# The last attention rebuilt: compressed branch in four batches, wide units in fours, state-space input projected earlier

## The chip, the cores and the metric

The kernel runs on one core of a Trainium2 chip. The metric is the device time of the whole kernel in microseconds (us), from which the median of several runs is taken. Five engines work side by side: TensorE (PE in the profile; PEld are its weight loads), VectorE (DVE), ScalarE (ACT), GpSimd (POOL) and SyncE (SP); the last two only start transfers here. They are joined by semaphores: an instruction waits until a counter has reached a number, and adds to one when it ends. Each engine takes its instructions strictly in the order of the program.

## The reference, cut to what matters

Three layers work on 512 positions of width 1024. The first two (attention with a position bias, then spatial gating, each followed by a feed-forward block) are not touched. The third joins an attention of eight heads in two key groups with a state-space recurrence. Each head has three branches: compressed (31 pooled keys), selected and window. With 512 positions there are 8 blocks and 16 may be selected, and the window is 512 wide, so both wide branches come to ordinary causal attention over up to 512 keys.

```python
q, kcr, vcr, ksl, vsl, kwn, vwn, z_a, g_br, u, z_s = split(h @ w_in)
kc = rms_norm(compress(kcr)); vc = compress(vcr)              # 31 pooled keys
for each head, each query t:
    p0 = masked_softmax(q . kc * scale, cmp_end <= t)         # compressed
    p1 = masked_softmax(rope(q) . rope(k_slc) * scale, causal)
    p2 = masked_softmax(rope(q) . rope(k_win) * scale, causal)
    o = g0 * p0 @ vc + g1 * p1 @ v_slc + g2 * p2 @ v_win
attn = o * silu(z_a)
y = s5_mixer(u)                                               # state space
y = gelu(y); y = y * sigmoid(y @ glu_w + glu_b)
out = x + gate * (concat(attn, y * silu(z_s)) @ w_out)
```

## The kernel before, in words

All weights come as slabs of 128x2048 numbers, in a fixed list: SP loads them into two buffers `w_raw`, ACT rounds each to `w_hi`, DVE takes the rest as `w_lo`, and TensorE multiplies three times (hi.hi, lo.hi, hi.lo; the helper `three`, L449). A slab of a projection gives two tiles of 128x512, each by 24 matmuls. ACT and DVE prepare one slab ahead.

The third layer begins with the projections of q and of the keys and values, then the compressed keys: `blocks`, two pairs of slabs, a small network (`hdn`), `kc_full`, the normalized keys `kcT`. Between those stand the slabs of the two gates, z_a (tile `za`) and z_s (`zs`): four slabs, eight tiles. Then ACT takes the silu of both.

The attention is one loop of steps in each of three engines (`attention`), over `UNITS_H`: 96 units (head pair i, group g, block of 128 queries it, branch br), the branch innermost. Of every three units one is compressed (br 0, 32 keys) and two are wide (128 * (it + 1) keys). At step s TensorE does the scores of unit s into bank s % 3 (L620), the transposes of the weights of unit s - 3 (L630) and the product with the values of unit s - 4 (L641). DVE adds the mask and finds the maximum (L1474, into `h_s`), inverts the row sum (L1482), multiplies it with the gate (L1965, `wbr`) and adds the result into `h_o` (L1970, L1973). ACT copies the transposed weights of unit s - 3 (L1062) and takes the exponential of unit s (L1070).

Beside the loop stands the projection of the state-space input u: two slabs, four tiles, at steps 0, 22, 44 and 66 (`SIDE_H`, helper `side`), all through bank 7 (`ps[7]`), with twelve turns of u into the layout of the recurrence (`U_STEPS`, L853) through the same bank. Whoever uses bank 7 waits for `side_free`, which the reader of the use before it raises. POOL waits for the last of these uses, then loads the tables of the first block of the recurrence into the place of h (L429), and those of the second when the attention has ended (`ho_done`).

After the loop h_o is transposed (L608) and gated, then four blocks of the recurrence follow (L871 to L885), the gate matrix, and the output projection. The attention of the first layer uses the same helpers over 64 units (head, it), all of them wide, with side work at every fourth step up to step 28 and none after.

Of the kernel before, what the change touches and what calls it, by code (L numbers as in the profile page):

```python
# [40 lines left out]
S_HU = S_HCV + 4  # L41
S_HGLU = S_HU + 2
S_HOUT = S_HGLU + 1
N_SLABS = S_HOUT + 4
ADA_TILES = 48
# [27 lines left out]
def program(nc, I, out, tab_d, tz_d):  # L73
    ctx = ExitStack()
    with ctx:
# [91 lines left out]
        h_p = at("h_p", 48 * K, [P, 4, T])  # L167
        h_pt = at("h_pt", 56 * K, [P, 3, T])
        h_s = at("h_s", 62 * K, [P, 3, T])
# [12 lines left out]
        h_mask = at("h_mask", 88 * K, [P, T])  # L182
        placed[0] = 93 * K
# [3 lines left out]
        kcT = seq("kcT", [P, CMP_PAD])  # L187
        vc = seq("vc", [CMP_PAD, H_GROUPS, HD])
        wbr = seq("wbr", [P, 4])
# [7 lines left out]
        posT = seq("posT", [P, 2, 32])  # L197
        w2c = seq("w2c", [P, 2, 2, HD])
# [5 lines left out]
        glu_b = seq("glu_b", [P, 4])  # L204
        gT = seq("gT", [N_BR * H_HEADS, T])
        hT = seq("hT", [2 * CMP_PAD, 2, 256])
        assert placed[0] <= 109 * K, placed
# [39 lines left out]
        U = at("U", 68 * K, [NCH, GB, L * CH])  # L247
# [64 lines left out]
        UNITS_H = [(i, g, it, br) for i in range(4) for g in range(H_GROUPS) for it in range(TT) for br in range(N_BR)]  # L312
# [19 lines left out]
        SIDE_A, SIDE_H = Side([4 * u for u in range(2 * TT)], TT), Side([22 * u for u in range(4)], 2)  # L332
        U_STEPS = {start + d: (b, part) for b, start in enumerate(SIDE_H.starts) for part, d in enumerate((4, 8, 12))}
        U_USES = len(U_STEPS)


        @block.sync
        def _(sp):
# [12 lines left out]
            with sp.Fori(1, N_SLABS // 2) as i:  # L351
# [10 lines left out]
        def _(gp):  # L362
# [71 lines left out]
        def _(pe):  # L434
# [350 lines left out]
            for i in range(4):  # L785
                transposes([h_qr[:, t, i * P:(i + 1) * P] for t in range(TT)], "hx_full")
            pe.wait_ge(sem("hk_done"), 1)
            for i in range(2):
                transposes([h_kr[:, t, i * P:(i + 1) * P] for t in range(TT)], "hx_full")

# [19 lines left out]
            b = bank()  # L810
# [27 lines left out]
            def beside_h(s):  # L838
                side(SIDE_H, s, pair_h)
                if s not in U_STEPS:  # L840
                    return
# [1323 lines left out]
```

## Time and profile before

| what | value |
|---|---|
| runs | 2027.04, 2044.36, 2056.81 us (median 2044.36) |
| profiled execution, its own time | 2040.69 us |
| span in its trace | 2038.9 us |
| what lies around the span | 1.8 us |
| mean granted TensorE clock | 0.946 |
| PE busy | 95% of the span |
| last attention, first score to the transposes of its result | 1664.48 to 1893.15 us |

The span runs from the first to the last instruction. PE is called busy for nearly all of it, but a matmul at half clock counts as busy too, and takes about twice as long, so the granted clock has to be read beside the busy share.

### The profile page before, as it was taken

How to read it: one execution, taken by the hardware profiler on the slowest of the kernel's cores; microseconds unless marked ns; L12 is line 12 of the kernel's file. 1: busy time of each engine (PE TensorE's matmuls, PEld its weight loads, DVE VectorE, ACT ScalarE, POOL GpSimd, SP SyncE). 2: the span in 40 equal slices, each digit the busy share in tenths (PEclk: the TensorE clock that was granted, in tenths of full speed). 3: DMA queues.
4: the chain of work that ended last, by engine and by line, in shares of the span. 5: the costliest groups of instructions: out<-in, count | busy, mean ns of one | idle time of the engine just before them, and what ended most of it. 6: DMA issues, size and time to landing. Idle time of an engine off the chain costs nothing.

```text
span 2038.9 us, 25450 instructions
## 1 busy us (share of the span) xinstructions
PE 1928.8 (95%) x9553; PEld 1586.3 (78%) x9553; DVE 1185.2 (58%) x2640; ACT 683.9 (34%) x1170; POOL 102.3 (5%) x198
## 2 busy tenths in 40 slices
PE   3999999999999999989999999999999899999769
PEld 3887778888888887778888888888887776676667
DVE  5775564876476565564434587657757843354442
ACT  3323563523332342232323342233233243353121
POOL 0001110001000001100000000100110000000000
PEclk9999999999999999999999999999999995595779
DMA  8344321435333436622222333634532320001401
GB/s 332 125 145 155 101 97 63 143 111 183 126 135 106 165 145 225 218 93 91 82 96 83 109 127 132 221 110 142 176 114 96 110 104 1 21 1 65 176 39 62
DMA packets 44405, 246.05 MB, mean 121 GB/s; under 512 B 6080, under 2 KB 6304, under 8 KB 25728
## 3 DMA queue, kind: packets, MB, share of 16 engines
q1 hardware_dynamic: 23200, 153.26, 21.2%
q0 software_dynamic: 21088, 91.21, 13.4%
q8 instruction: 76, 1.25, 0.3%
q14 instruction: 41, 0.34, 0.0%
HBM read 229.23 MB, written 15.22 MB: 120 GB/s over the span
## 4 chain that ended last, share of the span: by engine, by line
PE 83%; DVE 10%; DMA 3%; ACT 2%; issue 2%; SPq 0%; DVEq 0%; ACTq 0%
PE ps L449 63%; PE ps L620 6%; PE ps L641 5%; PE ps L630 4%; DMA ada_raw<-in_ada 3%; DVE w_lo L1300 2%; PE ps L759 1%; DVE ada_raw L1328 1%; ACT w_hi L915 1%; DMA bv_g<-in_bv_g 1%; PE ps L871 1%; DVE pre L1421 1%; PE ps L883 1%; PE ps L706 1%; PE ps L884 0%
## 5 line engine op out<-in xcount | busy, mean ns | idle before, releaser
L1300 DVE TENSOR_TENSOR w_lo<-w_raw,w_hi 128x2048 fp32r<-128x2048 f32 x136 | 311.6, 2291 | 149.5 <-ACT w_hi L915 149.2
L915 ACT ACTIVATE w_hi<-w_raw 128x2048 fp32r<-128x2048 f32 x136 | 260.0, 1913 | 399.6 <-PE ps L449 376.9
L449 PE MATMUL ps<-h_hi,w_hi 128*128 128x512 f32 (+1 forms) x1008 | 380.7, 378 | 11.9 <-issue 4.8
L449 PE MATMUL ps<-h_lo,w_hi 128*128 128x512 f32 (+1 forms) x1008 | 376.0, 373 | 0.0
L449 PE MATMUL ps<-h_hi,w_lo 128*128 128x512 f32 (+1 forms) x1008 | 375.6, 373 | 0.0
L449 PEld LDWEIGHTS ps<-h_hi,w_hi 128*128 128x128 f32 x1008 | 193.0, 191 | 46.2 <-issue 6.4
L449 PEld LDWEIGHTS ps<-h_hi,w_lo 128*128 128x128 f32 x1008 | 192.6, 191 | 32.8
L449 PEld LDWEIGHTS ps<-h_lo,w_hi 128*128 128x128 f32 x1008 | 192.9, 191 | 31.5
L449 PE MATMUL ps<-hid_hi,w_hi 128*128 128x512 f32 (+1 forms) x576 | 211.3, 367 | 0.0
L449 PE MATMUL ps<-hid_lo,w_hi 128*128 128x512 f32 (+1 forms) x576 | 210.5, 366 | 0.0
L449 PE MATMUL ps<-hid_hi,w_lo 128*128 128x512 f32 (+1 forms) x576 | 210.5, 366 | 0.0
L449 PE MATMUL ps<-w_hi,h_hi 128*128 128x512 f32 (+1 forms) x480 | 184.7, 385 | 13.6 <-DVE w_lo L1300 7.0
L449 PE MATMUL ps<-w_lo,h_hi 128*128 128x512 f32 (+1 forms) x480 | 182.2, 380 | 0.0
L449 PE MATMUL ps<-w_hi,h_lo 128*128 128x512 f32 (+1 forms) x480 | 182.1, 379 | 0.0
L1328 DVE CUSTOM_DVE_ANT_0 ada_raw<-ada_raw,cond 128x1024 f32<-128x1024 f32 x108 | 131.1, 1221 | 70.7 <-DMA ada_raw<-in_ada 69.6
L449 PEld LDWEIGHTS ps<-hid_hi,w_hi 128*128 128x128 f32 x576 | 108.6, 189 | 17.7
L449 PEld LDWEIGHTS ps<-hid_lo,w_hi 128*128 128x128 f32 x576 | 108.6, 189 | 17.5
L449 PEld LDWEIGHTS ps<-hid_hi,w_lo 128*128 128x128 f32 x576 | 108.6, 189 | 17.4
L449 PEld LDWEIGHTS ps<-w_hi,h_hi 128*128 128x128 f32 x480 | 92.1, 192 | 32.5 <-issue 10.5
L449 PEld LDWEIGHTS ps<-w_hi,h_lo 128*128 128x128 f32 x480 | 91.9, 191 | 16.8
L449 PEld LDWEIGHTS ps<-w_lo,h_hi 128*128 128x128 f32 x480 | 92.0, 192 | 16.1
L1352 DVE SCALAR_TENSOR_TENSOR xT<-ps,mod,xT 128x512 f32<-128x512 f32 x64 | 47.6, 749 | 94.4 <-PE ps L449 94.1
(359 smaller groups left out, 2763.4 us busy)
## 6 DMA issues: line engine op xcount, KB each, us to landing
w_raw<-in_slabs SPq DMA_DIRECT2D x136, 1024.0 KB, 4.8
ada_raw<-in_ada POOLq DMA_DIRECT2D x108, 512.0 KB, 4.6
s_tables<-s_tab POOLq DMA_DIRECT2D x4, 2692.0 KB, 9.5
s_t<-s_tables POOLq DMA_DIRECT2D x4, 2692.0 KB, 9.5
ada_first<-in_ada SPq DMA_DIRECT2D x4, 1536.0 KB, 18.3
a_bias<-in_a_bias POOLq DMA_DIRECT2D x16, 256.0 KB, 3.0
xT<-in_xT SPq DMA_DIRECT2D x1, 2048.0 KB, 19.9
s_toeplitz<-KTp POOLq DMA_DIRECT2D x32, 64.0 KB, 3.5
```

Source lines behind the costliest of these rows:

```text
L449: last = mm(o, l, r, start=start and n == 0, stop=stop and n == 2)
L620: mm(ps[s % 3][:, 0:n], q, k, start=True, stop=True).then_inc(sem(pre + "s_full"), 1)
L630: last = nc.tensor.transpose(b[0:w, j:j + P], pt[:, u % 4, j:j + w], ident[:])
L641: last = mm(ps[5 + u % 2][:, 0:HD], pt[0:w, u % 3, j * P:(j + 1) * P], value(units[u], j), start=j == 0, stop=j == nb - 1)
L706: last = mm(norm_banks[t // 2][1][:, t % 2:t % 2 + 1], sq_x[:, k % 2, t * P:(t + 1) * P], ones[:, 0:1], start=k == 0 and t % 2 == 0, stop= ...
L759: last = mm(b[:, t * P:(t + 1) * P], b_v[:, t, gm * P:(gm + 1) * P], b_ws[:, gm // 3, :], start=True, stop=True)
L871: last = mm(b[:, g * NCH:(g + 1) * NCH], t["Gt"][:, g, q * P:(q + 1) * P], UT[:, blk * GB + g, :], start=True, stop=True)
L883: mm(o, UT[:, blk * GB + g, :], Tz[blk % 2][:, g, :], start=True, stop=False)
L915: A(w_hi[s][:], w_raw[:, s, :], ACT.Copy).then_inc(sem("hi_done"), 1)
L1300: tt(w_lo[s][:], w_raw[:, s, :], w_hi[s][:].bitcast(F32), ALU.subtract).then_inc(sem("lo_done"), 1)
L1328: V.tensor_tensor_reduce(out=w, in0=w, in1=cond[:, which, :], scale=1.0, scalar=0.0, op0=ALU.mult, op1=ALU.add, accum_out=mod_s[:, o:o + 1 ...
L1352: free(stt(xT[:, o, :], b[:], mod[:, g + o:g + o + 1], xT[:, o, :], ALU.mult, ALU.add))
```

## The change

It rebuilds the last attention and moves the slabs around it.

- The compressed branch leaves the units. `UNITS_H` becomes 64 wide units, four in a row with the same it (two branches, two groups). For each head pair i one batch (`compressed`) does the compressed branch for both groups and all 512 queries, in three parts at the steps of `CMP_STEPS`: scores against `kblk`, a matrix with the keys of the two groups in its two halves; two transposes; the product with `vblk`, the values laid out in blocks. All through bank 7. DVE does the softmax's sums for all eight query and group blocks at once, and adds the result to `h_o` at the steps of `CMP_ADD`.
- The scores of two units, the two groups, are issued together at every even step. DVE writes the masked scores into `h_p` itself, which has five places, so `h_s` is gone, and ACT's exponential works in place.
- The results of four units lie side by side in one bank. One reciprocal, one product with the gates (`h_w`), one multiplication and one addition serve all four.
- u is projected before the attention, where z_a and part of z_s were, and only three slabs stand there instead of four. The other half of z_a and all of z_s come beside the attention: three slabs, six tiles, at steps 1, 11, 22, 33, 44 and 55. SP's list `H_SLABS` gives the new order of loads.
- The silu of `za` is taken at step 13, that of `zs` after the attention. POOL's first load of tables waits for the last projection beside the loop (`H_READ`), its second for `h_added`.

```diff
-        UNITS_H = [(i, g, it, br) for i in range(4) for g in range(H_GROUPS) for it in range(TT) for br in range(N_BR)]
+        UNITS_H = [(i, it, br, g) for i in range(4) for it in range(TT) for br in (1, 2) for g in range(H_GROUPS)]
...
-        SIDE_A, SIDE_H = Side([4 * u for u in range(2 * TT)], TT), Side([22 * u for u in range(4)], 2)
-        U_STEPS = {start + d: (b, part) for b, start in enumerate(SIDE_H.starts) for part, d in enumerate((4, 8, 12))}
+        SIDE_A, SIDE_H = Side([4 * u for u in range(2 * TT)], TT), Side([1, 11, 22, 33, 44, 55], 2)
+        KCT_STEP = 4
+        U_STEPS = {step: (n // 3, n % 3) for n, step in enumerate((15, 16, 17, 19, 20, 21, 24, 25, 26, 28, 29, 30))}
+        CMP_STEPS = {step: (n // 3, n % 3) for n, step in enumerate((6, 9, 13, 23, 27, 31, 35, 38, 41, 46, 50, 57))}
+        CMP_ADD = {16 * i + 22: i for i in range(4)}
+        ZA_STEP = SIDE_H.starts[1] + 2
...
+            for n, slab in enumerate(H_SLABS):
+                sp.wait_ge(sem("lo_done"), S_HQ + n - 1)
+                sp.dma_start(w_raw[:, n % 2, :], I["slabs"][S_HQ + slab]).then_inc(sem(f"raw_in{n % 2}"), 16)
...
-                    gp.wait_ge(sem("side_free"), len(SIDE_A.starts) + len(SIDE_H.starts) + U_USES)
+                    gp.wait_ge(sem("side_free"), H_READ)
                 elif b == 1:
-                    gp.wait_ge(sem("ho_done"), NUH)
+                    gp.wait_ge(sem("h_added"), 4)
...
-            slab_t(H)
-            pe.wait_ge(sem("kcn_done"), 1)
-            transposes([kcn[:].rearrange("n g d -> n (g d)")], "kct_full")
-            pe.wait_ge(sem("acc_free"), c("bank"))
...
+            def compressed(i, part):
+
+                pe.wait_ge(sem("side_free"), base[0])
+                base[0] += 1
+                if part == 0:
+                    for it in range(TT):
+                        last = mm(ps[7][:, 64 * it:64 * it + 64], hq[:, i, it * P:(it + 1) * P], kblk[:], start=True, stop=True)
+                    last.then_inc(sem("c_full"), 1)
+                elif part == 1:
+                    pe.wait_ge(sem("c_exp"), i + 1)
+                    for h in range(2):
+                        last = nc.tensor.transpose(ps[7][:, h * P:(h + 1) * P], c_s[:, h * P:(h + 1) * P], ident[:])
+                    last.then_inc(sem("c_turned"), 1)
+                else:
+                    for h in range(2):
+                        last = mm(ps[7][:, 256 * h:256 * h + 256], c_pt[:, h, :], vblk[:], start=True, stop=True)
+                    last.then_inc(sem("c_out"), 1)
+
+            for s in range(NUH + 4):
+                if s < NUH and s % 2 == 0:
+                    i, it, br, _ = UNITS_H[s]
+                    n, ts = P * (it + 1), slice(it * P, (it + 1) * P)
+                    if s >= 2:
+                        pe.wait_ge(sem("hs_done"), s - 1)
+                    for g in range(H_GROUPS):
+                        r = slice(HD * g, HD * g + HD)
+                        last = mm(ps[(s + g) % 3][:, 0:n], hqr[r, i, ts], hk[r, br - 1, 0:n], start=True, stop=True)
+                    last.then_inc(sem("hs_full"), 1)
...
+                    for j in range(it + 1):
+                        last = mm(o, h_pt[:, u % 3, j * P:(j + 1) * P], hv[:, j, vc], start=j == 0, stop=j == it)
...
-            act.wait_ge(sem("z_copied"), 1)
-            A(za[:], za[:], ACT.Silu).then_inc(sem("z_done"), 1)
-            A(zs[:], zs[:], ACT.Silu).then_inc(sem("z_done"), 1)
...
+                if s == ZA_STEP:
+                    act.wait_ge(sem("side_free"), ZA_READ)
+                    A(za[:], za[:], ACT.Silu).then_inc(sem("za_done"), 1)
...
+            act.wait_ge(sem("side_free"), SIDE_ALL)
+            A(zs[:], zs[:], ACT.Silu).then_inc(sem("zs_done"), 1)
...
+                    step(tt(h_q4[:], ps[5 + q % 2][:, 0:256].rearrange("p (j d) -> p j d", d=HD),
+                            h_w[:, q % 2, :, :].rearrange("p b g -> p (b g)").unsqueeze(2).to_broadcast([P, 4, HD]), ALU.mult))
+                    tt(h_o[:, it, i * P:(i + 1) * P].rearrange("p (g d) -> p g d", d=HD), h_q4[:, 0:2, :], h_q4[:, 2:4, :], ALU.add)\
+                      .then_inc(sem("ho_done"), 1)
```

What the three engines then have in a row is shown at two places. The first is TensorE in the middle of the loop. Of before, the steps 8 to 10, where the units go from 384 to 512 keys (kcT and vc are compressed, hk and hv wide):

```order
L620 MATMUL ps<-hk,hqr 128x384
L630 MATMUL ps<-ident,h_p 128x128 x2
L641 MATMUL ps<-hv,h_pt 128x64 x2
L853 MATMUL ps<-ident,uT 64x128 x4
L620 MATMUL ps<-kcT,hq 128x32
L630 MATMUL ps<-ident,h_p 32x128
L641 MATMUL ps<-hv,h_pt 128x64 x2
L620 MATMUL ps<-hk,hqr 128x512
```

The same place of the changed kernel, steps 13 to 17 (vblk is the compressed batch, L852 are turns of u):

```order
L901 MATMUL ps<-hv,h_pt 128x64 x3
L871 MATMUL ps<-vblk,c_pt 128x256 x2
L882 MATMUL ps<-hk,hqr 128x512 x2
L891 MATMUL ps<-ident,h_p 128x128 x3
L901 MATMUL ps<-hv,h_pt 128x64 x3
L891 MATMUL ps<-ident,h_p 128x128 x4
L901 MATMUL ps<-hv,h_pt 128x64 x3
L852 MATMUL ps<-ident,uT 64x128 x4
L882 MATMUL ps<-hk,hqr 128x128 x2
L891 MATMUL ps<-ident,h_p 128x128 x4
L901 MATMUL ps<-hv,h_pt 128x64 x4
L852 MATMUL ps<-ident,uT 64x128 x4
```

The compressed units are gone from between the wide ones, two scores stand together, and turns of u stand at steps next to each other.

The second place is ACT at the beginning of the loop. Of before, from the root of the compressed keys' norm (kst) on:

```order
L1245 ACTIVATE kst<-kst,eps 32x2
L915 ACTIVATE w_hi_54<-w_raw 128x2048
L1249 ACT_TABLE_LOAD
L1249 ACTIVATE za<-za 128x2048
L1250 ACTIVATE zs<-zs 128x2048
L915 ACTIVATE w_hi<-w_raw 128x2048
L1070 ACT_TABLE_LOAD
L1070 ACTIVATE h_p,row_sum<-h_s,neg_max 128x32
```

Of the changed kernel, from the same instruction on, and further down around the silu of za:

```order
L1301 ACTIVATE kst<-kst,eps 32x2
L1333 ACT_TABLE_LOAD
L1333 ACTIVATE h_p,row_sum<-h_p,neg_max 128x128
L971 ACTIVATE w_hi_54<-w_raw 128x2048
...
L1320 ACT_TABLE_LOAD
L1320 ACTIVATE za<-za 128x2048
L1327 ACTIVATE h_pt<-ps 128x384
L1333 ACT_TABLE_LOAD
L1333 ACTIVATE h_p,row_sum<-h_p,neg_max 128x512
```

The two silus no longer stand ahead of the first exponential; one of them stands in the middle of the loop, with a table load on each side.

## Rows read from the trace of the kernel before

**Rows 1.** The page: engines' busy time, the granted clock in 40 slices, the chain.

```profile
PE 1928.8 (95%) x9553; PEld 1586.3 (78%) x9553; DVE 1185.2 (58%) x2640; ACT 683.9 (34%) x1170; POOL 102.3 (5%) x198
...
PEclk9999999999999999999999999999999995595779
...
PE 83%; DVE 10%; DMA 3%; ACT 2%; issue 2%; SPq 0%; DVEq 0%; ACTq 0%
```

**Rows 2.** Windows by stage: projections, last slab, last attention, rest (first row: columns).

```profile
core 0: us, PE busy (x) PEld busy (x) DVE busy (x) ACT busy (x) POOL busy (x), PEclk, DMA share, GB/s
...
1653.00:1664.50 11.50, 10.66 (x49) 8.47 (x47) 5.05 (x9) 3.60 (x4) 0.00 (x0) 1.00 0.26 93
1664.50:1893.15 228.65, 227.32 (x929) 157.72 (x929) 94.02 (x482) 98.45 (x309) 1.06 (x2) 0.68 0.07 24
1893.15:2038.90 145.75, 110.78 (x608) 97.83 (x608) 55.61 (x94) 24.83 (x30) 3.15 (x6) 0.84 0.25 97
```

**Rows 3.** Windows, same columns: the first attention, then where the clock fell or rose.

```profile
244.00:300.00 56.00, 56.00 (x325) 38.98 (x323) 37.65 (x154) 35.02 (x103) 7.46 (x14) 1.00 0.31 104
1672.00:1674.00 2.00, 1.49 (x6) 0.90 (x7) 1.39 (x11) 1.64 (x10) 0.00 (x0) 0.98 0.40 74
1674.00:1676.00 2.00, 2.00 (x7) 0.89 (x7) 0.28 (x1) 0.96 (x3) 0.00 (x0) 0.50 0.90 377
...
1724.00:1726.00 2.00, 2.00 (x8) 1.56 (x7) 0.00 (x0) 0.00 (x0) 0.00 (x0) 0.72 0.00 0
1738.00:1740.00 2.00, 2.00 (x10) 1.49 (x11) 1.64 (x10) 1.26 (x5) 0.00 (x0) 0.69 0.00 0
1778.00:1780.00 2.00, 2.00 (x6) 1.61 (x7) 1.97 (x3) 0.47 (x2) 0.00 (x0) 0.57 0.00 0
1840.00:1842.00 2.00, 2.00 (x14) 1.12 (x13) 0.98 (x7) 1.33 (x6) 0.22 (x1) 0.79 0.01 4
```

**Rows 4.** PE in order of time (start, us, instruction): first attention, one round of four.

```profile
252.96 0.49 PE L620 MATMUL ps<-a_kT,a_qT 64*128 64x128 f32 x2
...
259.60 0.48 PE L620 MATMUL ps<-a_kT,a_qT 64*128 64x128 f32 x2
```

**Rows 5.** PE in order of time, last attention: half clock, then full clock.

```profile
1693.61 0.63 PE L620 MATMUL ps<-kcT,hq 64*128 64x32 f32 x2
...
1715.41 0.63 PE L620 MATMUL ps<-kcT,hq 64*128 64x32 f32 x2
...
1789.43 0.40 PE L620 MATMUL ps<-kcT,hq 64*128 64x32 f32 x2
...
1790.50 0.60 PE L853 MATMUL ps<-ident,uT 128*64 128x128 f32 x4
1791.03 0.49 PE L620 MATMUL ps<-hk,hqr 64*128 64x128 f32 x2
...
1802.94 0.36 PE L620 MATMUL ps<-kcT,hq 64*128 64x32 f32 x2
```

**Rows 6.** PE in order of time: start of the attention, side work begun at half clock.

```profile
1652.30 0.50 PE L449 MATMUL ps<-h_hi,w_hi 128*128 128x512 f32 x1
...
1664.48 0.40 PE L620 MATMUL ps<-kcT,hq 64*128 64x32 f32 x2 [0.84 <-DVE kcT L1952]
1664.82 0.50 PE L449 MATMUL ps<-h_hi,w_hi 128*128 128x512 f32 x1
...
1670.48 0.71 PE L620 MATMUL ps<-hk,hqr 64*128 64x128 f32 x4
...
1720.50 0.80 PE L449 MATMUL ps<-h_hi,w_hi 128*128 128x512 f32 x1
...
1728.29 1.12 PE L620 MATMUL ps<-hk,hqr 64*128 64x512 f32 x2
```

**Rows 7.** ACT in order of time: start of the attention, side copy, after the attention.

```profile
1664.29 1.92 ACT L1249 ACTIVATE za<-za 128x2048 f32<-128x2048 f32 x1 [7.35 <-DVEq L1950]
...
1669.82 1.28 ACT L1070 ACT_TABLE_LOAD   x1
...
1728.40 0.60 ACT L1038 ACTIVATE uT<-ps 128x512 f32<-128x512 f32 x1 [7.22 <-PE ps L449]
...
1910.31 0.59 ACT L1262 ACTIVATE y_nat<-ps 64x512 f32<-64x512 f32 x1 [9.66 <-PE ps L885]
```

**Rows 8.** POOL in order of time: the loads of the first two tables.

```profile
1841.78 0.54 POOL L429 DMA_DIRECT2D s_t<-s_tables  x1 [336.59 <-ACT UT L1046]
...
1893.39 0.53 POOL L429 DMA_DIRECT2D s_t<-s_tables  x1 [50.54 <-DVE h_o L1973]
```

**Rows 9.** Groups of PE's instructions, 244 to 300 us: the scores (busy us, mean ns).

```profile
L620 PE MATMUL ps<-a_kT,a_qT 64*128 64x512 f32 (+3 forms) x66 | 26.8, 486 | 0.0
```

More of the change, by code:

```diff
@@ L789, in _ @@
                 transposes([h_kr[:, t, i * P:(i + 1) * P] for t in range(TT)], "hx_full")
+            for i in range(4):
+                transposes([h_qr[:, t, i * P:(i + 1) * P] for t in range(TT)], "hx_full")
             for kind in range(2):
@@ L809, in _ @@
             pe.wait_ge(sem("hdn_done"), 2)
-            b = bank()
+            pe.wait_ge(sem("acc_free"), c("bank"))
+            wait(pe, "side_free", base[0])
+            base[0] += 1
             for kind in range(2):
@@ L836, in pair_h, with turn_u @@
                 return ps[7][:], (w_hi[sl][:, cols], w_lo[sl][:, cols]), (h_hi[:, k, :], h_lo[:, k, :]), False
[L838 to L841, printed above, removed]
-                b, part = U_STEPS[s]
+            def turn_u(b, part):
                 pe.wait_ge(sem("side_free"), base[0])
@@ new lines, in _ @@
+            for s in range(NUH + 4):
[8 more added lines that the diff above has]
+                    last.then_inc(sem("hs_full"), 1)
+                u = s - 3
+                if 0 <= u < NUH:
+                    n = P * (UNITS_H[u][1] + 1)
+                    pe.wait_ge(sem("hp_ready"), u + 1)
+                    if u >= 2:
+                        pe.wait_ge(sem("hpt_ready"), u - 1)
+                    for j in range(0, n, P):
+                        last = nc.tensor.transpose(ps[3 + u % 2][:, j:j + P], h_p[:, u % 5, j:j + P], ident[:])
+                    last.then_inc(sem("ht_full"), 1)
+                u = s - 4
+                if 0 <= u < NUH:
+                    i, it, br, g = UNITS_H[u]
+                    pe.wait_ge(sem("hpt_ready"), u + 1)
+                    if u % 4 == 0 and u >= 8:
+                        pe.wait_ge(sem("ho_done"), u // 4 - 1)
+                    o, vc = ps[5 + u // 4 % 2][:, (u % 4) * HD:(u % 4 + 1) * HD], slice((br - 1) * P + g * HD, (br - 1) * P + (g + 1) * HD)
+                    for j in range(it + 1):
+                        last = mm(o, h_pt[:, u % 3, j * P:(j + 1) * P], hv[:, j, vc], start=j == 0, stop=j == it)
+                    last.then_inc(sem("ho_full"), 1)
+                side(SIDE_H, s, pair_h)
+                if s == KCT_STEP:
+                    pe.wait_ge(sem("kcn_done"), 1)
+                    pe.wait_ge(sem("side_free"), base[0])
+                    base[0] += 1
+                    nc.tensor.transpose(ps[7][:, 0:CMP_PAD], kcn[:].rearrange("n g d -> n (g d)"), ident[0:CMP_PAD, 0:CMP_PAD])\
+                      .then_inc(sem("kct_full"), 1)
+                if s in U_STEPS:
+                    turn_u(*U_STEPS[s])
+                if s in CMP_STEPS:
+                    compressed(*CMP_STEPS[s])
@@ L1976, in _ @@
-            attention(UNITS_H, lambda u: CMP_PAD if u[3] == 0 else P * (u[2] + 1), mask_h, combine_h, "h", SIDE_H)
-            c.add("slab", 2)
-            c.add("full", 2)
-            dve.wait_ge(sem("z_done"), 2)
-            dve.wait_ge(sem("ho_done"), NUH)
+            kc = ps[7][0:CMP_PAD, :].rearrange("n (k g d) -> n k g d", k=4, d=HD)
+            step(cp(kcn[:], kc[:, 0, :, :]), *[cp(vblk[CMP_PAD * r:CMP_PAD * (r + 1), r, :], kc[:, 1, r % 2, :]) for r in range(4)])
+            V.engine_nop().then_inc(sem("side_free"), 1)
@@ L1981, in _ @@
+            c.add("slab", 3)
+            c.add("full", 3)
+            dve.wait_ge(sem("za_done"), 1)
             for i in range(5):
```

199 lines of the change are left out of this document (131 added, 68 removed).

## Prediction

> **What bounds the kernel now.** I read the page first [rows 1]: PE is busy for 95% of the span and makes up 83% of the chain that ended last, so the time is set by what PE is given and how fast it runs it. The slices of the granted clock are nines except for a run near the end, 5595779. The windows by stage [rows 2] say what that run is: the last attention, 228.65 us, in which PE is busy for 227.32 us at a mean granted clock of 0.68. DVE (94.02) and ACT (98.45) are far from being the bound there. With two levels, 1.00 and 0.50, a mean of 0.68 means that 64% of the stage ran at half clock. So there are two ways to make this stage shorter: less work for PE, or the same work at full clock. The change touches both. The slab ahead of the loop, 11.50 us at 1.00, belongs to the place as well. The rest, 145.75 us, does not change.
>
> Then I looked at where the clock moves [rows 3]. It fell at about 1674, after a start with waits on PE (0.84 us in front of the first score [rows 6]); it rose near 1725, some 4.5 us into the side work that began at 1720.50; it fell again near 1739, some 10 us after that work; it rose near 1780, again during side work, and fell once more in the window at 1840. Between the side works nothing raised it. But the first attention, 56 us of which are in [rows 3], has no side work there and is made of wide units alone, and it holds 1.00. So in the last attention it is not the lack of side work by itself that costs the clock; the narrow compressed units, a third of its units, are the plain difference.
>
> **PE's work after, at full clock.** Wide units: one round of four of the first attention (128, 256, 384, 512 keys) takes 259.60 - 252.96 = 6.64 us [rows 4]. The changed loop has 64 wide units with the same mix, 16 rounds: 106.2 us. As a check on before: nine units took 1802.94 - 1789.43 = 13.51 us at full clock with three turns of u, and 21.80 at half clock with one [rows 5]. A turn is 1791.03 - 1790.50 = 0.53; without turns that is 11.9 against some 20.8 (one turn of 0.95 taken off), a factor of 1.76, by which I price half clock below. Side work: 1670.48 - 1664.82 = 5.66 us at full clock, 7.79 when begun at half [rows 6]; six of them are 34.0 us. Two are new inside the loop, and the slab of 11.50 us ahead of it is what they replace, so this is a move and no saving. Turns: 12 x 0.53 = 6.4 us, as before. Compressed batches: no row shows one. It is four scores, two transposes and two products. From below, each costs no more than one 32-key score (0.36 [rows 5]): 8 x 0.36 = 2.9 us; from above, the two products, of 256 columns each, cost twice that: 3.6. I take 3.0, since scores and transposes are as short as in that row and the products stream only a little longer; 12 us for four, 11.6 to 14.4 for the range. They replace 32 compressed units, whose scores alone cost more than 32 x 0.36 = 11.5. kcT: 0.3. The sum is 106.2 + 34.0 + 6.4 + 12.0 + 0.3 = 158.9 us.
>
> **Waits.** The first score starts when the slab ahead of it is gone. Before, that slab ran from 1652.30, and kcT with its wait came behind it, to 1664.48 [rows 6]. After, the network's product goes to bank 7 and waits for the copy of the last slab's tile, below 1 us, so I start the loop at 1653.2. The start: before, ACT spent 1.92 us on the silu of za at 1664.29, as much on zs, and 1.28 on a table load at 1669.82 [rows 7], all ahead of the first exponential. Now the two silus are gone from there, and what stays is mask, table load, exponential, copy: I put 3 us on PE for this. The silu of za at step 13 costs ACT 1.28 + 1.92 + 1.28 = 4.5 us, with copies and exponentials queued behind it. The exponentials run three steps ahead of the transposes, and three steps of 384 to 512 keys are over 5 us, so I cost it at nothing, 2 us if that cover is short. The silu of zs falls into ACT's idle 9.66 us before 1910.31 [rows 7]: nothing. POOL's first load of tables moves from 1841.78 to behind the side work of step 55; 12 steps follow, over 20 us, and its wait in POOL's queue has nothing behind it but the second load, which is issued at the end as before, at 1893.39 [rows 8]. Nothing. SP's new order of slabs keeps two buffers and the same spacing of one slab per 22 steps. Nothing.
>
> Bank 7 is now used by turns, batches, kcT and side work, 31 times against 16. Each user waits for the reader of the one before. The reader of a side use before was ACT, 0.60 us at 1728.40 [rows 7]; turns of u stand at neighbouring steps, so one read has a step to be done in, and a step is 6.64 / 4 = 1.7 us. Bounds: 0 and 0.6 us for each of the 31, or 0 to 19; I take 4, since most have a step or more between them. At the end the last four results need two DVE operations and the addition of the compressed part before h_o can be turned: 1.5 us. Waits: 3 + 4 + 1.5 = 8.5, range 3 to 25.
>
> **The clock.** With 159 us of work and 1.00 throughout, the stage would be 167.4 us. The first attention says that wide units hold the clock [rows 3]; side work now comes every 11 steps, some 18 us, and before it raised the clock each time. But the start has waits again, and before, the clock fell there. And three places (steps 16 to 21 and their like) put scores of 128 keys, turns and batches close together. I take two stretches at half clock, each until the next side work, about 10 us of full-clock work: 10 x 0.76 = 7.6 us, and 7.79 - 5.66 = 2.1 for the side work begun at half, 9.7 each, 20 in all. The stage is then 187 us at a mean clock of about 0.88.
>
> **Sum.** Loop from 1653.2 to 1653.2 + 187.4 = 1840.6, against 1893.15: 52.5 us less. The profiled execution took 2040.69, so 1988. The median of the runs shown is 2044.36, 0.2% above it, which is below what a measurement tells apart; 2% here is 41 us.
>
> **A rule on the scores.** No row shows the scores of the two groups next to each other, each on one half of the array's rows. The scores take 26.8 of 56 us in the first attention [rows 9], so 3.2 us of a round and 51 in all; two at once throughout would save 25 us, none nothing. Every score is two instructions (x2 in [rows 4]), in order, so only the second of one and the first of the next can meet: a quarter, 13 us. In my sum they are in series, since the trace shows no other case. The Trainium skill, TensorEngine Tiling (Array Packing), section Key Properties, says that different tiles can execute weight loads and matmuls in parallel; by that rule the sum would be some 1975, and nothing in this case's trace bears on it yet. It is the third rival.
>
> **Rivals.**
> - The clock holds throughout. For it: the first attention [rows 3]. Against: its banks and queues were not shared with turns and batches. 20 us less: 1968. Chance 0.17.
> - Half clock as often as before, 64% of the stage. For it: the clock stayed down for 50 and 40 us between rises [rows 3], the start still waits. At 1.76 the 167.4 us of work and waits become 167.4 / (1 - 0.64 x 0.432) = 231, the end 1884: 2032, no change that can be told. Chance 0.15.
> - The scores overlap: 13 us less than the forecast, 1975, and with a clock that holds 1955. Chance 0.17.
> - Slower: bank 7 becomes the chain. Its 31 uses each cost a full round trip, TensorE to the reader and back, behind exponentials in ACT's queue or in DVE's; at 2.5 us each that is 78 us, PE idles, and the clock stays down: 231 + 78 - 4 = 305, less 240 from 1653.2 to 1893.15, gives 65 more, 2106. From about 1.7 us for each use, with the clock down, it is slower by over 2%. Against: the one read shown took 0.60 us [rows 7] and a step is longer. Chance 0.05.
> - The forecast, one to three stretches at half clock, 1978 to 2003: chance 0.46.
>
> **How the numbers follow.** Faster by over 2% (below 2003) are the forecast, the first and the third rival, less the upper edge of the forecast's bounds (waits to 25 us, batches at 14.4): 0.74. Within 2% are the second rival and that edge: 0.21. Slower: 0.05. The range holds all but the slow rival, most of the second, and the overlap with a held clock: 1960 to 2024.
>
> **What the trace after would show.** The first score near 1653; the transposes of h_o near 1841; a stage of 187 us at a clock near 0.88, low at the start and in one place further on; rounds of four at 6.6 us where the clock is full; no wait of PE for ACT at step 13 or for POOL's tables; waits for bank 7 below 0.6 us each; the rest at 146 us. Two scores of different groups that begin within less than their length would show the overlap. I am wrong if the clock stays at 0.50 between side works although the narrow units are gone, or if PE shows waits of over a microsecond for bank 7.

## The result and the profile after

The changed kernel takes 1942.38 us (median of four runs, 1941.69 to 1943.64) against 2042.61: a ratio of 0.956, 95% interval 0.951 to 0.961. It is faster, as forecast, but by about 99 us between the two profiled executions (2040.69 and 1941.69) where 52.5 were forecast, and the time lies below the range, 1960 to 2024.

The page after, in the parts that answer to [rows 1]:

```profile
PE 1823.2 (94%) x9449; PEld 1525.6 (79%) x9449; DVE 1154.1 (59%) x2392; ACT 669.9 (35%) x1086; POOL 101.9 (5%) x198
...
PEclk9999999999999999999999999999999999999789
...
PE 80%; DVE 11%; DMA 4%; ACT 2%; issue 2%; SPq 0%; DVEq 0%; ACTq 0%
```

PE is as busy as before by its share (94%), and the bound as before. But the slices of the clock that read 5595 in [rows 1] are nines now. The windows by stage after, with the columns of [rows 2]: up to the first score, the last attention up to the transposes of its result, the rest.

```profile
1560.00:1656.49 96.49, 88.40 (x462) 71.69 (x461) 72.88 (x95) 25.52 (x22) 0.00 (x0) 0.98 0.31 113
1656.49:1795.53 139.04, 129.92 (x875) 101.83 (x873) 68.03 (x243) 85.11 (x226) 1.06 (x2) 1.00 0.13 47
1795.53:1939.90 144.37, 109.85 (x608) 97.42 (x608) 55.53 (x94) 27.86 (x32) 3.14 (x6) 0.85 0.26 98
```

The stage takes 139.04 us at 1.00, where 187.4 at about 0.88 were forecast. The rest is 144.37 us against 145.75 [rows 2]. So the whole surprise lies in this one stage. PE in order of time shows half of it (start, duration, instruction; x4 are the two scores of a pair, two instructions each):

```profile
1743.43 0.92 PE L882 MATMUL ps<-hk,hqr 64*128 64x384 f32 x4
1744.28 0.44 PE L891 MATMUL ps<-ident,h_p 128*128 128x128 f32 x2
...
1749.05 1.13 PE L882 MATMUL ps<-hk,hqr 64*128 64x512 f32 x4
1750.11 0.55 PE L891 MATMUL ps<-ident,h_p 128*128 128x128 f32 x3
```

Start to start, two scores of 512 keys take 1750.11 - 1749.05 = 1.06 us and two of 384 keys 0.85. In the kernel before, one score of 512 keys at full clock took 1788.33 - 1787.28 = 1.05 us:

```profile
1787.28 1.12 PE L620 MATMUL ps<-hk,hqr 64*128 64x512 f32 x2
1788.33 0.55 PE L630 MATMUL ps<-ident,h_p 128*128 128x128 f32 x3
```

Two scores now cost what one did.

PE's idle time in the stage is 139.04 - 129.92 = 9.1 us, where I had put 8.5 of waits. The rows with the longest waits (the bracket: idle before, and who ended it):

```profile
1657.95 0.47 PE L465 MATMUL ps<-h_hi,w_hi 128*128 128x512 f32 x1 [0.97 <-DVEq L2027]
1664.95 0.70 PE L882 MATMUL ps<-hk,hqr 64*128 64x256 f32 x4 [0.64 <-DVE neg_max L2039]
1686.28 0.88 PE L901 MATMUL ps<-hv,h_pt 128*128 128x64 f32 x6 [0.85 <-ACT h_pt L1327]
1688.78 0.88 PE L901 MATMUL ps<-hv,h_pt 128*128 128x64 f32 x6 [1.18 <-ACT h_pt L1327]
1702.70 0.47 PE L465 MATMUL ps<-h_hi,w_hi 128*128 128x512 f32 x1 [1.40 <-ACT UT L1102]
1795.53 2.82 PE L624 MATMUL ps<-ident,h_o 128*128 128x128 f32 x16 [1.64 <-DVE h_o L2101]
```

And what ACT does ahead of the two waits near 1687: the silu of za between two table loads.

```profile
1681.43 0.49 ACT L1327 ACTIVATE h_pt<-ps 128x384 f32<-128x384 f32 x1 [0.94 <-PE ps L891]
...
1682.64 1.28 ACT L1320 ACT_TABLE_LOAD   x1
1683.94 1.91 ACT L1320 ACTIVATE za<-za 128x2048 f32<-128x2048 f32 x1
1685.76 0.47 ACT L1327 ACTIVATE h_pt<-ps 128x384 f32<-128x384 f32 x1
1686.24 1.28 ACT L1333 ACT_TABLE_LOAD   x1
```

### The profile page after: what moved, and what is told of

It is laid out like the page before. It is cut to its first block, busy times and chain, and to the rows that moved or that the text cites. A ratio compares the mean times of both kernels' runs of the same rounds, so it can differ in the third digit from the quotient of the medians.

```text
span 1939.9 us, 24528 instructions
## 1 busy us (share of the span) xinstructions
PE 1823.2 (94%) x9449; PEld 1525.6 (79%) x9449; DVE 1154.1 (59%) x2392; ACT 669.9 (35%) x1086; POOL 101.9 (5%) x198
## 4 chain that ended last, share of the span: by engine, by line
PE 80%; DVE 11%; DMA 4%; ACT 2%; issue 2%; SPq 0%; DVEq 0%; ACTq 0%
PE ps L465 66%; DMA ada_raw<-in_ada 3%; DVE w_lo L1384 3%; PE ps L636 2%; PE ps L657 2%; PE ps L901 2%; PE ps L646 1%; DMA ada_first<-in_ada 1%; DVE ada_raw L1412 1%; PE ps L775 1%; PE ps L882 1%; PE ps L891 1%; ACT w_hi L971 1%; PE ps L939 1%; PE ps L927 1%
```

## The experiments

Two questions: why do the scores cost half, and what had brought the clock down? Where a time is set against another, the profile's window of the loop stands below, with the columns of [rows 2]; the eighth number is the granted clock.

**1. Pairs on the same half.** The units are put in another order, so that a pair is the two branches of one group:

```diff
-UNITS_H = [(i, it, br, g) for i .. for it .. for br in (1, 2) for g in range(H_GROUPS)]
+UNITS_H = [(i, it, br, g) for i .. for it .. for g in range(H_GROUPS) for br in (1, 2)]
...
-    for g in range(H_GROUPS):
+    for b in range(2):
```

> The changed kernel, but the two scores of a pair belong to the two branches of one group, so both use the same half of the array's rows. Number of scores, their sizes and their places stay. Theory: two scores of different groups run at the same time, since after the change four instructions of 512 columns take 1.06 us, and in the first attention before two took 1.05. Then the scores cost 20.8 us more (45.5 against 24.7 us) and the kernel comes to 1963 us. Rival: pairing only halves the number of changes between score and transpose, and what is saved is saved by that: then the time stays at 1942 us. Clock in the stage 1.00 by both.

**2. One score at each step.**

```diff
-if s < NUH and s % 2 == 0:
+if s < NUH:
...
-    for g in range(H_GROUPS):
-        last = mm(ps[(s + g) % 3][:, 0:n], hqr[r, i, ts], hk[r, br - 1, 0:n], start=True, stop=True)
+    last = mm(ps[s % 3][:, 0:n], hqr[r, i, ts], hk[r, br - 1, 0:n], start=True, stop=True)
```

> The changed kernel with one score at each step, in place of two at every second one; groups alternate, with transposes and value products between. Theory (overlap of neighbours): nothing is left to overlap, 1963 us, and 1 to 3 us more if each change between 64-row and 128-row instructions costs something. Rival (scores of different groups overlap wherever they stand): 1942 us.

Measured: 1961.79 us (1953.76 to 1974.23) for the first, 1969.98 (1967.47 to 1973.57) for the second. The first median stands near the 1963 us expected partly by luck: of its four runs two took 1953.76 and 1955.61 us, at mean clocks of 0.977 and 0.978 over the kernel (the changed kernel has 0.978), and two 1967.97 and 1974.23 at 0.972 and 0.968. PE at full clock in the first, then in the second:

```profile
1769.90 1.98 PE L882 MATMUL ps<-hk,hqr 64*128 64x512 f32 x4
1771.81 0.55 PE L891 MATMUL ps<-ident,h_p 128*128 128x128 f32 x3
```

```profile
1768.88 1.12 PE L881 MATMUL ps<-hk,hqr 64*128 64x512 f32 x2
1769.93 0.55 PE L890 MATMUL ps<-ident,h_p 128*128 128x128 f32 x3
```

Two scores of 512 keys cost 2 x 1.05 = 2.10 us when each stands alone, 1.91 when they are neighbours on the same half of the rows, 1.06 when they are neighbours on different halves. So 0.85 of the 1.04 us saved per pair is overlap, which settles it, and 0.19 comes from standing side by side at all (the rival has that much). Over the 32 pairs, with 0.63, 0.84 and 1.05 us for one score of 256, 384 and 512 keys in the second run, 0.41 for 128 in the kernel before and 0.42, 0.64, 0.85 and 1.06 for a pair after: 16 x 2.93 = 46.9 us against 8 x 2.97 = 23.8. Pairs on one half take 0.64, 1.06, 1.49 and 1.91 us: 8 x 5.10 = 40.8. Of the 23.1 us saved, 17.0 are overlap and 6.1 standing side by side. The loops of the two runs, and in each a stretch in which the clock fell:

```profile
1654.89:1822.13 167.24, 160.34 (x875) 122.34 (x873) 68.18 (x243) 85.98 (x226) 1.06 (x2) 0.91 0.11 39
1664.00:1688.00 24.00, 24.00 (x82) 17.57 (x81) 7.66 (x33) 8.52 (x28) 0.00 (x0) 0.57 0.12 44
```

```profile
1656.30:1823.80 167.50, 162.54 (x876) 116.49 (x874) 68.57 (x243) 86.94 (x226) 1.06 (x2) 0.94 0.11 39
1664.00:1688.00 24.00, 23.60 (x75) 15.48 (x75) 9.00 (x39) 9.12 (x32) 0.00 (x0) 0.57 0.12 44
```

The second loop is 167.50 - 139.04 = 28.5 us longer than the changed one. The scores are 23.1 of that; the stretch at half clock is some 9 (an estimate: a mean of 0.57 is 86% of 24 us at half clock, taken at the prediction's factor of 1.76); and PE is idle for 5.0 us in place of 9.1, which gives 4 back. The fall I had not expected: pairs on different halves seem to help to keep the clock up. It is no rule, since two of the four runs of the first have next to no fall, and run 4 below has falls in spite of such pairs.

**3. The kernel before without compressed units.**

```diff
-UNITS_H = [.. for it in range(TT) for br in range(N_BR)]
+UNITS_H = [.. for it in range(TT) for br in (1, 2)]
...
-Side([22 * u for u in range(4)], 2)
+Side([16 * u for u in range(4)], 2)
```

> The kernel before without its compressed units, so that only the 64 wide units are left; side work at every 16th step in place of every 22nd, to fit. The compressed branch is missing from the output. Theory: the narrow units brought the clock down. Then the stage runs at a clock of 0.95 to 1.00 and takes 16 x 6.64 + 4 x 5.66 + 6.4 + about 6 of waits = 141 us, the kernel about 1954 us. Rival: the waits at the start and the distance between side works bring it down: a mean clock near 0.7, a stage of 190 us or more, the kernel above 2000 us.

Measured: 1949.35 us (1949.09 to 1965.85), ratio to before 0.961 (0.955 to 0.967). Its attention:

```profile
1668.66:1802.47 133.81, 133.13 (x769) 95.23 (x769) 69.45 (x322) 81.09 (x213) 1.06 (x2) 1.00 0.10 38
```

Single scores, the old loop, the same 0.84 us of wait in front of its first score, and a clock of 1.00. The compressed units had brought it down. (The run of 1965.85 us has a mean clock of 0.970 over the kernel, the other three 0.980, so a fall can come here too.) The side work stands at other steps as well; run 13 below has it at the same steps, and there the clock falls.

**4. The first attention in pairs too**, two heads of a tile at every even step, `a_bias` with four places:

```diff
-UNITS_A = [(h, it) for h in range(A_HEADS) for it in range(TT)]
+UNITS_A = [(2 * i + g, it) for i in range(A_HEADS // 2) for it in range(TT) for g in range(2)]
...
-    if s < U:
...
-        mm(ps[s % 3][:, 0:n], q, k, start=True, stop=True).then_inc(sem(pre + "s_full"), 1)
+    if s < U and s % 2 == 0:
+        for g in range(2):
...
+            last = mm(ps[(s + g) % 3][:, 0:n], q, k, start=True, stop=True)
```

> The changed kernel, with the first attention paired in the same way: the two heads that share a tile, one on each half of the rows, have their scores issued together at every even step; four places for the position bias in place of three. Theory (overlap): its 64 scores cost 45.5 us in series and half of that in pairs, so 1942 - 21 = 1921 us. Rival: DVE, busy for 37.65 of 56 us there, or the bias loads become the bound and the gain is under 8 us.

Measured: 1924.22 us (1922.09 to 1929.43), ratio to before 0.945 (0.942 to 0.949), 18 us less than the changed kernel, where 21 were expected, and the fastest version here. A little goes to waits of PE for ACT (3.9 us in its first attention, one of them below). In the profiled execution, 1929.43 us, the clock fell too: from about 289 to 296 us, in the paired first attention, and in the last attention, whose instructions are those of the changed kernel, to a mean of 0.96 (last line), 4.5 us more than 139.04.

```profile
257.74 0.88 PE L659 MATMUL ps<-a_v,a_pt 128*128 128x64 f32 x6 [0.72 <-ACT a_pt L1120]
...
261.57 0.92 PE L637 MATMUL ps<-a_kT,a_qT 64*128 64x384 f32 x4
262.42 0.33 PE L648 MATMUL ps<-ident,a_p 128*128 128x128 f32 x1
...
1639.69:1783.27 143.58, 134.48 (x875) 105.47 (x874) 68.02 (x243) 85.28 (x226) 1.06 (x2) 0.96 0.13 46
```

**5. Narrow work put back into the changed kernel**, three instructions at one step, results unread:

```diff
+if s % 2 == 1 and 9 <= s < NUH + 3:
+    mm(idle[:, 256:288], hq[r, s // 16 % 4, 0:P], kblk[r, 32 * g:32 * (g + 1)], start=True, stop=True)
...
+    nc.tensor.transpose(idle[0:32, 320:448], h_p[:, u % 5, 0:32], ident[:])
...
+    mm(idle[:, 448:512], h_pt[0:32, u % 3, 0:P], vblk[0:32, 0, :], start=True, stop=True)
```

> The changed kernel with narrow work added that leads nowhere: at every odd step from 9 to 65 TensorE also does a score of 32 keys, a transpose of 32 columns and a product from 32 partitions, as a compressed unit of the kernel before did; nobody reads the results, and no engine has more to do. 29 such units at about 0.63 us (before at full clock: nine units in 11.85 us, six of them wide ones at 6.64 / 4 each) are 18 us. Theory (narrow instructions bring the clock down by themselves): a mean clock of 0.65 to 0.8 in the stage and 1942 + 18 + 30 to 60 = 1990 to 2020 us. Rival (it takes their chain through DVE and ACT, or unpaired scores, or the rare side work): the clock stays above 0.95 and the time is 1960 us.

**6. All side work early.**

```diff
-Side([1, 11, 22, 33, 44, 55], 2)
+Side([1, 5, 10, 14, 18, 22], 2)
```

> The changed kernel with all its side work in the first third: steps 1, 5, 10, 14, 18 and 22 in place of 1 to 55, so that some 75 us of the loop have none. Theory (wide units hold the clock by themselves): clock 1.00 in that stretch, 1942 to 1945 us. Rival (the step of the prediction: between side works the clock falls until the next one): it falls in the long stretch and stays down, 20 to 30 us more, 1962 to 1972 us.

**7. The silus of the kernel before taken later.**

```diff
-A(za[:], za[:], ACT.Silu).then_inc(sem("z_done"), 1)
-A(zs[:], zs[:], ACT.Silu).then_inc(sem("z_done"), 1)
...
+if pre == "h" and s in (40, 62):
...
+    A((za if s == 40 else zs)[:], (za if s == 40 else zs)[:], ACT.Silu).then_inc(sem("z_done"), 1)
```

> The kernel before with the two silus of the gates taken at steps 40 and 62 in place of ahead of the loop. Theory (narrow units bring the clock down wherever they are): the fall at the start goes or comes some us later, the mean clock of the stage stays between 0.6 and 0.8, and the time is that of before less at most 10 us. Rival (the waits at the start bring it down, and it stays down until the next side work): no fall in the first 50 us, some 20 us less than before.

Measured: 1972.72 us (1971.31 to 1981.53), 1947.98 (1945.96 to 1948.87) and 2040.51 (ratio to before 1.0005, 0.996 to 1.005). The windows of the loops of 5 and 6, and a stretch of 7:

```profile
1659.55:1825.03 165.48, 161.00 (x1020) 122.67 (x1019) 68.08 (x243) 87.44 (x226) 1.06 (x2) 0.99 0.11 40
```

```profile
1654.98:1800.36 145.38, 135.73 (x875) 106.12 (x873) 67.90 (x243) 84.97 (x226) 1.06 (x2) 0.95 0.13 45
```

```profile
1674.00:1718.00 44.00, 44.00 (x141) 29.69 (x141) 14.67 (x77) 14.65 (x49) 0.00 (x0) 0.50 0.00 1
```

In 5 my theory fell: narrow instructions alone, among pairs, do not bring the clock down. Their price is above the 0.63 us of the expectation: the loop is 165.48 - 139.04 = 26.4 us longer, 0.91 for each of the 29 units, and the rest of the 30.3 us between the medians lies ahead of the loop and behind it. In 6 neither time came: the clock fell three times for 3 to 7 us, only once of these (1758 to 1762) in the long stretch without side work, and each time it came back by itself or with side work; the time is 5.6 us longer. In 7 the old kernel's clock falls near 1674 with no silu ahead of the loop and only one wait of PE at its start, 0.84 us in front of the first score. Run 3 has that wait too and holds 1.00, so the waits at the start were not the cause.

**8 to 11. Two or three of these together**, in the changed kernel: single scores (as in 2) with the narrow work of 5; pairs with narrow work and early side work; all three; single scores with early side work.

> The changed kernel with both undone at once as far as TensorE sees it: one score at each step (as in the run with single scores) and the added narrow work that leads nowhere (as in that run). Each alone left the clock at or near 1.00 for nearly all of the stage. Theory now (what brings the clock down is the two together, narrow instructions among scores that do not overlap): a mean clock of 0.65 to 0.85 in the stage, and 1970 + 30 for the narrow work + 20 to 60 = 2020 to 2060 us. Rival (the compressed units' own chain through DVE and ACT, or the rare side work of the kernel before): the clock stays above 0.93 and the time is the sum of the two, 2000 us.

> Paired scores, the added narrow work that leads nowhere, and all side work in the first third. Theory (rare side work matters once narrow instructions are there): in the long stretch without side work the clock falls and stays down for tens of us, 1973 + 20 to 40 = 1993 to 2013 us. Rival (pairs hold it, side work or not): short falls at most, as without the narrow work, 1973 to 1982 us.

> Single scores, the added narrow work that leads nowhere, and all side work in the first third, in the changed kernel. Single scores with narrow work and spread side work held the clock, pairs with narrow work and early side work too. Theory (it takes all three: then the clock falls and nothing raises it): a fall in the long stretch without side work that lasts over 20 us, and 1993 + 15 to 60 = 2008 to 2053 us. Rival (what the changed loop does still differs in another way): falls of 10 us at most, 1993 to 2003 us.

> Single scores and early side work without the narrow work. Theory (narrow instructions are one of the three that it takes): falls of 10 us at most, as in the first attention, which has single wide scores and no side work from 244 to 300 us at 1.00; 1970 to 1980 us. Rival (single scores without side work are enough): falls of over 20 us, 1985 us or more.

Measured: 1992.90 us (1990.14 to 1998.19), 1974.92 (1972.48 to 1977.33), 2013.51 (1988.19 to 2021.93) and 1966.46 (1964.73 to 1971.52). The loop of the first; then, of the third, two stretches behind its last side work, which ends near 1745:

```profile
1659.57:1840.99 181.42, 177.55 (x1020) 129.13 (x1019) 68.69 (x243) 87.71 (x226) 1.06 (x2) 0.98 0.10 37
```

```profile
1740.00:1814.00 74.00, 73.71 (x456) 53.52 (x454) 29.32 (x111) 35.33 (x101) 1.06 (x2) 1.00 0.12 45
1816.00:1870.00 54.00, 53.18 (x173) 36.81 (x173) 11.39 (x40) 13.06 (x36) 0.00 (x0) 0.50 0.00 1
```

The theory of 8 fell too: single scores and three narrow instructions at one step hold 0.98 while side work is spread. In 10 the theory came true in three of four runs: they took 2011.66, 2015.36 and 2021.93 us, at mean clocks of 0.965 to 0.955 over the kernel, and one took 1988.19 at 0.978. In the profiled one, 2021.93 us, the clock held for some 70 us without side work and then stayed at half until the loop ended. So three narrow instructions at one step among single scores can bring the clock down as well, where no side work follows, but not every time. With pairs (9, where the rival came) or without narrow work (11, where the theory did), early side work costs nothing that can be told here, though the clock has falls of up to 10 us in both.

**12. More work in the kernel before**: 24 matmuls of 128x512 at four steps between its side works.

```diff
+if s in (11, 33, 55, 77):
...
+    for k in range(24):
+        mm(ps[7][:], h_hi[:, k % KT, 0:P], h_lo[:, k % KT, :], start=True, stop=True)
```

> The kernel before with more work: at steps 11, 33, 55 and 77 of its last attention TensorE also does 24 matmuls of 128x512 into bank 7, of the kind of the side work, whose result nobody reads. They cost 4 x 5.66 = 22.6 us at full clock. Theory (the clock stays down in that kernel because its narrow, single units do not raise it again and side work is rare): with side work at every 11th step the stage's mean clock rises from 0.68 to 0.9 or more, and the kernel gets faster by doing more, 2030 + 23 - 40 to 80 = 1975 to 2015 us. Rival (side work only happens to stand near the rises): the clock stays near 0.7 and the time is 2050 to 2060 us.

Measured: 2040.43 us, ratio 1.003 (0.999 to 1.006): 22.6 us of added work for nothing, but no gain either.

```profile
1663.00:1893.72 230.72, 228.96 (x1024) 161.80 (x1024) 94.04 (x484) 98.50 (x309) 1.06 (x2) 0.79 0.07 24
```

Neither time came. The mean clock of the stage is higher than before (0.79 against 0.68), but it does not stay up: it rises during two of the four added blocks (near 1694 and 1793), is up already at the other two, and falls again some 9, 12 and 3 us behind the first, second and fourth, the last time until the loop ends. Rare side work was a part of it, not the root.

**13. The old row of instructions without its chain.** The kernel of 3 with the narrow instructions of the kernel before in their old places (a product at even steps, a score and a transpose at odd ones), read by nobody:

```diff
+if narrow and s % 2 == 0:
+    mm(idle[:, 448:512], pt[0:32, u % 3, 0:P], vc[:, 0, :], start=True, stop=True)
...
+if narrow and s % 2 == 1:
+    mm(idle[:, 256:288], hq[r, s // 16 % 4, 0:P], kcT[r, :], start=True, stop=True)
+    last = nc.tensor.transpose(idle[0:32, 320:448], h_p[:, (s - 3) % 4, 0:32], ident[:])
```

> The kernel before without its compressed units, as run already (clock 1.00 in the stage, 1949 us), plus narrow work that leads nowhere, in the order in which that kernel had it: a product from 32 partitions at every even step from 8 to 64, a score of 32 keys and a transpose of 32 columns at every odd one. TensorE's row of instructions is then nearly that of the kernel before; DVE and ACT have only the wide units. 29 units at 0.9 us are 26 us. The compressed branch is missing from the output. Theory (that row of instructions brings the clock down): a mean clock of 0.65 to 0.85 in the stage, 2000 to 2040 us. Rival (the compressed units' own chain through DVE and ACT does, by waits too short for the profile to list): the clock stays above 0.95, 1975 us.

**14 and 15. The same places in the changed loop**, with pairs and with single scores.

> The changed kernel, scores in pairs, with the narrow work that leads nowhere in the order in which the run that brought the clock down had it: the product from 32 partitions at even steps, the score of 32 keys and the transpose of 32 columns at odd ones, 29 units. Theory (the order decides, since three narrow instructions at one step did not bring the clock down): a mean clock below 0.85 in the stage, 1972 + 20 to 50 = 1992 to 2022 us. Rival (pairs and side work at every 11th step hold the clock, whatever the order): above 0.95, 1972 us.

> The same narrow work in the same order, and one score at each step. Theory (order, or order and single scores together): a mean clock below 0.85, 1993 + 20 to 60 = 2013 to 2053 us. Rival (side work at every 11th step, or the units by fours, hold it): above 0.95, 1993 to 2000 us.

Measured: 13 took 2006.59 to 2067.61 us, the fall lasting longer in some runs than in others, so it has no ratio; its fastest run is still 57 us above the kernel of 3, at a mean clock of 0.964 over the kernel against 0.980. By these two clocks some 66 us more are at half clock, which at the factor 1.76 is half of the 57 us (an estimate); the added units are the rest. 14 took 1975.79 us (1969.58 to 1985.85), 15 2018.28 us (2014.24 to 2019.88). The loop of 13, in its execution of 2067.61 us; 14; then 15 and in it the longest stretch at half clock:

```profile
1667.05:1921.59 254.54, 253.86 (x914) 173.25 (x914) 69.46 (x322) 81.09 (x213) 1.06 (x2) 0.61 0.06 22
```

```profile
1655.92:1822.12 166.20, 161.95 (x1020) 124.76 (x1019) 68.10 (x243) 87.04 (x226) 1.06 (x2) 0.98 0.11 40
```

```profile
1661.58:1872.99 211.41, 208.26 (x1020) 146.52 (x1019) 68.83 (x243) 88.13 (x226) 1.06 (x2) 0.87 0.09 31
...
1772.00:1804.00 32.00, 32.00 (x90) 19.66 (x90) 11.51 (x35) 10.31 (x27) 0.00 (x0) 0.50 0.03 5
```

PE is busy for the whole of that stretch, 32.00 of 32.00 us, and at half clock. 13 and 15 went the way of their theories (15 with 0.87, a little above the 0.85 named), 14 the way of its rival. In 13 it is the row of TensorE's instructions alone that does it: DVE and ACT do no more than in 3. In 14 the same narrow work in the same places, beside pairs, costs what it cost in 5 (1975.79 against 1972.72) and the clock holds. In 15, beside single scores, it costs 42 us more than in 14, 23 for the scores and the rest for the clock.

## Why the prediction was wrong

The mechanism was right: TensorE is the bound, the stage has less work and runs at a higher clock, and the rest of the kernel does not move. Two terms of the sum failed: the scores, put in series, and the 20 us for two stretches at half clock. They make up 43 of the 46 us between 1988 and 1941.69.

**The scores.** "In my sum they are in series, since the trace shows no other case." They overlap, and whole: 46.9 us in series, 23.8 in pairs, 23.1 less (runs 1 and 2). The rival on this had the right event and the wrong price: "only the second of one and the first of the next can meet: a quarter, 13 us". That was argued from the order of four instructions; the bound that I worked out beside it, half of the scores, is nearly what came. And the trace of the kernel before did show another case, which I overlooked. A turn of u (eight transposes from rows 0 to 63) stands there next to a score of the second group, on the other half, at half clock:

```profile
1695.68 0.79 PE L853 MATMUL ps<-ident,U 64*128 64x64 f32 x5
1696.16 0.58 PE L620 MATMUL ps<-hk,hqr 64*128 64x128 f32 x1
1696.27 0.52 PE L853 MATMUL ps<-ident,U 64*128 64x64 f32 x3
1696.54 0.42 PE L620 MATMUL ps<-hk,hqr 64*128 64x128 f32 x1
1696.89 1.11 PE L630 MATMUL ps<-ident,h_p 128*128 128x128 f32 x4
```

The score begins ahead of the last three transposes, and both take 1696.89 - 1695.68 = 1.21 us, where such a turn in front of a score of the first group takes 1752.87 - 1751.96 = 0.91 and such a score alone 1699.27 - 1698.54 = 0.73. So something in the trace did bear on the overlap, against "nothing in this case's trace bears on it yet". The Trainium skill, TensorEngine Tiling (Array Packing), section Key Properties (different tiles can run weight loads and matmuls in parallel) is borne out: 1.06 us for two scores on two halves against 1.91 on one.

**The clock.** "I take two stretches at half clock", 20 us: there were none in the stage; the window reads 1.00. The step behind it was that the clock falls after the waits at the start and stays down until the next side work. Runs 7 and 3 show that the waits at the start do not matter much, run 6 that among pairs a fall can end by itself without side work. What I took for the plain difference to the first attention, the narrow units, was the right culprit for the kernel before (run 3: 1.00 without them), but only together with single scores (runs 14 and 15), and in the places where they stood (runs 8 and 15) or with no side work behind them (run 10). The change takes away both, and either did for most of it (run 3 without narrow units: 1.00; run 14 with pairs: 0.98). At 64% of 228.65 us and the factor 1.76, the half clock had cost the kernel before some 63 us, the largest part of the 99 (an estimate).

**The compressed batches** were put at 12 us. Their three groups of instructions in the stage:

```profile
L871 PE MATMUL ps<-vblk,c_pt 128*128 128x256 f32 x16 | 4.3, 393 | 0.0
L862 PE MATMUL ps<-kblk,hq 128*128 128x64 f32 x32 | 4.3, 276 | 0.3 <-ACT zs L1094 0.3
L867 PE MATMUL ps<-ident,c_s 128*128 128x128 f32 x8 | 1.6, 279 | 0.0
```

That is 10.2 us busy, and start to start, as some of it overlaps, about 9.4 (four times some 1.0, 0.35 and 1.0): 2 to 3 us too much, and below my lower bound of 11.6. That bound stood on "each costs no more than one 32-key score", which bounds from above and not "from below". What they replace, put at more than 11.5 us, was worth some 29 at full clock (an estimate: 32 units at the 0.91 us of run 5).

**Waits:** 8.5 forecast, 9.1 measured; that the sums agree is in part luck, since the parts differ. The start took 0.64 where I had 3, with the side work of step 1 between the first score and what follows from it. Bank 7 cost 3.5 us in five waits where I had 4: 0.97 for the network's product at the start, 0.51, twice 0.30, and 1.40 for the last turn of a block right ahead of side work. That one is over the microsecond which I had named as a sign of being wrong, but it weighs little. The silu of za, which I "cost at nothing, 2 us if that cover is short", was 0.85 + 1.18 = 2.0: the exponentials run three steps ahead, but both waits are for `h_pt`, ACT's copy of the transposed weights, which is made only one step before the product that reads it. ACT was not behind: it had waited 0.94 us for PE in front of the copy at 1681.43, and made the next one behind the silu, at 1685.76. The end was 1.64 (1.5), and three more waits for `h_pt` make 1.1. The slower rival, bank 7 as the chain, is far off.

**The start** was forecast at 1653.2 and came at 1656.49, 3.3 us late. No run shows that the new order does this: runs 1, 2, 5, 6, 8 to 11, 14 and 15 share all that stands ahead of the loop with the changed kernel, and their first scores come between 1652.28 (run 11) and 1661.58 (run 15).

By these, 187.4 - 20 (clock) - 23.1 (scores) - 3 (batches) + 0.6 (waits) = 141.9, against 139.04; no run takes the last 3 us apart. SP's order, the zs silu and POOL's loads of tables were hidden, as said: the second load is issued at 1795.77, with the end of the attention.

What stays open is why the place of narrow instructions decides. Three at one step (run 8, 0.98) and the same three spread over two steps (run 15, 0.87) differ in one thing that the traces show: in every second unit of run 8 the narrow score belongs to the other half of the rows than the wide one beside it and runs within its time. Here the wide score with the narrow one in it takes 1739.12 - 1738.07 = 1.05 us, as much as alone:

```profile
1738.07 0.69 PE L881 MATMUL ps<-hk,hqr 64*128 64x512 f32 x1
1738.08 0.41 PE L888 MATMUL ps<-kblk,hq 64*128 64x32 f32 x2
1738.60 0.59 PE L881 MATMUL ps<-hk,hqr 64*128 64x512 f32 x1
1739.12 0.55 PE L896 MATMUL ps<-ident,h_p 128*128 128x128 f32 x3
```

Whether that is what holds the clock, no run shows.

## What to carry to other kernels

Where a contraction fills only 64 of 128 rows, put two such matmuls of different halves next to each other in TensorE's row: here each such pair cost what one had cost (1.06 us against 1.05), and it paid in the first attention as well (1942 to 1924 us). Read the granted clock of a stage beside its busy share before counting instructions, and when it is low, take out one kind of instruction at a time, with nothing else changed, to find which one lowers it. A bound that is worked out from rows belongs in the forecast at its full size, unless a row speaks against it.

## What was unexpected of the hardware

A TensorE that is busy for 32.00 of 32.00 us can be at half clock all that time (run 15), and 254 us at a mean of 0.61 (run 13). Doing more can cost nothing: 96 matmuls of 128x512 added to the kernel before left its time at a ratio of 1.003, as the mean clock of the stage was higher with them (0.79 against 0.68).
